# A two-block transformer on one core: ScalarE splits the second weight panel of the next stage ahead of a norm's squares or root instead of behind its root

## The reference

```python
def first_block(x, ...):                 # "a" in the kernel
    for l in range(2):
        h = rmsnorm(x, g_mix[l]); z = h @ w_in[l]          # attention, retention, gates
        x = x + mixed @ w_out[l]
        h2 = rmsnorm(x, g_mlp[l])
        x = x + square(relu(h2 @ w_up[l])) @ w_down[l]
    return rmsnorm(x, g_final)

def second_block(x, ...):                # "b" in the kernel
    for l in range(2):
        y = hybrid_mixer(x, ...)                           # sparse attention, gated linear attention
        x = layer_norm(DN_ALPHA * x + y, ln1_g[l], ln1_b[l])
        y = conv_ffn(x, w_up_2[l], conv_w[l], conv_b[l], w_down_2[l])
        x = layer_norm(DN_ALPHA * x + y, ln2_g[l], ln2_b[l])
    return x
```

## Time and profile before

| | |
|---|---|
| time, median of 3 runs | 3656.37 us (3656.33 to 3658.37) |
| profiled execution: time, span | 3656.84 us, 3655.0 us |
| TensorE matmul busy | 3461.4 us (95%) |
| ScalarE, VectorE, GpSimd busy | 1434.5, 1582.4, 1452.4 us (39, 43, 40%) |
| mean granted TensorE clock | 0.977 |

### The profile page before, as it was taken

One profiled execution on the slowest core, in us unless ns is written; L12 is line 12 of the kernel. 1 busy time (PEld: TensorE's weight loads), 2 busy tenths in 40 slices (PEclk: granted clock), 3 DMA queues, 4 the chain that ended last, 5 costly groups with the idle time before them and its releaser, 6 DMA issues.

```text
span 3655.0 us, 45462 instructions
## 1 busy us (share of the span) xinstructions
PE 3461.4 (95%) x16338; PEld 2807.0 (77%) x16338; DVE 1582.4 (43%) x2423; ACT 1434.5 (39%) x2116; POOL 1452.4 (40%) x1100
## 2 busy tenths in 40 slices
PE   7999999999999999999889999999897899999997
PEld 5788778887788778887668876787676688767875
DVE  5624242226623432237842444434577414344345
ACT  4735232224734332323363444333343524343333
POOL 3334444444334444444313343444332233434442
PEclk9999999999999999999999999999998999999999
DMA  3122222222112222222112221222221121212221
GB/s 139 58 74 77 92 92 93 93 103 81 70 70 93 92 82 102 92 98 78 70 35 73 69 93 70 92 97 98 72 78 58 44 72 70 93 58 96 99 92 58
DMA packets 43812, 298.49 MB, mean 82 GB/s; under 512 B 4816, under 2 KB 5456, under 8 KB 8592
## 3 DMA queue, kind: packets, MB, share of 16 engines
q1 hardware_dynamic: 41696, 291.52, 22.3%
q10 hardware_dynamic: 1968, 4.94, 0.4%
HBM read 294.34 MB, written 2.10 MB: 81 GB/s over the span
## 4 chain that ended last, share of the span: by engine, by line
issue 56%; POOL 33%; PE 8%; DVE 1%; ACT 1%; POOLq 1%; DVEq 0%; ACTq 0%
POOL w_lo L310 33%; PE ps L424 3%; PE ps L426 3%; PE ps L425 3%; POOLq L305 0%; PE ps L506 0%; DVE arena L1627 0%; ACT arena L1100 0%; POOLq L309 0%; DVE x L1662 0%; DVE arena L1650 0%; ACT y_hi L1119 0%; DVE tmp L1455 0%; ACT x L1418 0%; DVE x L1899 0%
## 5 line engine op out<-in xcount | busy, mean ns | idle before, releaser
L310 POOL TENSOR_TENSOR w_lo<-w_raw,w_hi 128x512 fp32r<-128x512 f32 x1096 | 1452.2, 1357 | 2161.0 <-ACT w_hi L924 2161.0
L424 PE MATMUL ps<-x_hi,w_hi 128*128 128x512 f32 x2752 | 1095.9, 398 | 20.6 <-DVE x_lo L1440 15.7
L426 PE MATMUL ps<-x_hi,w_lo 128*128 128x512 f32 x2752 | 1078.8, 392 | 0.0
L425 PE MATMUL ps<-x_lo,w_hi 128*128 128x512 f32 x2752 | 1077.8, 392 | 0.0
L924 ACT ACTIVATE w_hi<-w_raw 128x1024 fp32r<-128x1024 f32 x548 | 547.6, 1048 | 509.3 <-PE ps L426 509.3
L424 PEld LDWEIGHTS ps<-x_hi,w_hi 128*128 128x128 f32 x2752 | 521.4, 189 | 148.9 <-issue 24.3
L426 PEld LDWEIGHTS ps<-x_hi,w_lo 128*128 128x128 f32 x2752 | 520.1, 189 | 110.7
L425 PEld LDWEIGHTS ps<-x_lo,w_hi 128*128 128x128 f32 x2752 | 521.3, 189 | 106.7 <-issue 2.4
L424 PE MATMUL ps<-y_hi,w_hi 128*128 128x512 f32 x1248 | 493.4, 395 | 19.5 <-DVE x L1662 13.0
L425 PE MATMUL ps<-y_lo,w_hi 128*128 128x512 f32 x1248 | 489.3, 392 | 0.0
L426 PE MATMUL ps<-y_hi,w_lo 128*128 128x512 f32 x1248 | 488.8, 392 | 0.0
(11 more groups left out here) (184 smaller groups left out, 3153.5 us busy)
## 6 DMA issues: line engine op xcount, KB each, us to landing
w_raw<-stream SPq DMA_DIRECT2D x274, 1024.0 KB, 4.8
x<-x_t SPq DMA_DIRECT2D x4, 512.0 KB, 5.5
rotary<-rot ACTq DMA_DIRECT2D x4, 512.0 KB, 3.6
y_t<-x SPq DMA_DIRECT2D x8, 256.0 KB, 2.1
ct<-consts ACTq DMA_DIRECT2D x2, 770.0 KB, 4.9
arena<-pos ACTq DMA_DIRECT2D x2, 256.0 KB, 3.5
vec<-vectors ACTq DMA_DIRECT2D x4, 116.0 KB, 2.0
ct<-consts ACTq DMA_DIRECT2D x1, 128.0 KB, 3.9
```

What stands on the lines that cost most here:

```text
L310: ins = nc.gpsimd.tensor_tensor(WL[:, s, c:c + S], RAW[:, s, c:c + S], WH[:, s, c:c + S].bitcast(F32), ALU.subtract)
L424: pe.matmul(ps, wh, xh, start=(k == 0), stop=False)
L425: pe.matmul(ps, wh, xl, start=False, stop=False)
L426: return pe.matmul(ps, wl, xh, start=False, stop=last)
```

## The change

In `norm` (first block, five places) `hi(second_panel)` moves from behind `token_root` to ahead of it. In the layer norms (second block, three places: the fourth has no next stage) `hi` of the second panel moves from behind `root` to ahead of the eight squares. No instruction is added or removed; VectorE's, TensorE's, GpSimd's and SyncE's programs are the same.

```diff
@@ -1161,8 +1161,8 @@
                     const_dma(act, CT[:, 256:CW], consts_in[0, :, 256:CW], "consts_a")
                     hi(0)
                 warm_root()
+                hi(second_panel)
                 token_root(bank, (t, l, which + "_ms"), (t, l, which + "_root"))
-                hi(second_panel)
                 for k in range(KD):
                     src = X[:, k, :] if to_x else TMP[:, k % 2, :]
@@ -1405,13 +1405,13 @@
                 for which, gain in (("ln1", VB["ln1_g"]), ("ln2", VB["ln2_g"])):
+                    if which == "ln1" or l + 1 < DEPTH:
+                        hi(w["ff"] + 1 if which == "ln1" else at_b(l + 1)["iq"] + 1)
                     for _ in squares(lambda k: X[:, k, :], KD, lambda k: TMP[:, k % 2, :], lambda k: (t, l, which + "_centered", k),
                             lambda k: (t, l, which + "_ms", k - 2) if k >= 2 else None, (t, l, which + "_sq")):
                         pass
                     warm_root()
                     root(PS[:, 5, :], D, LN_EPS, (t, l, which + "_root"), [(t, l, which + "_ms"), "eps"])
-                    if which == "ln1" or l + 1 < DEPTH:
-                        hi(w["ff"] + 1 if which == "ln1" else at_b(l + 1)["iq"] + 1)
                     for k in range(KD):
```

## The result

| | median, us | runs | lowest to highest |
|---|---|---|---|
| before | 3656.35 | 12 | 3654.75 to 3661.80 |
| changed | 3665.98 | 12 | 3664.03 to 3668.14 |

A forecast was written before the change was run, and what follows sets the result against it. It took the ScalarE-VectorE chain on which TensorE waits in the nine norms as the bound. RMS norms +5.7 and layer norms -1.2 gave +4.5 us, so 3660.9 us, 0.12% above, range 3656.5 to 3666.0.

The forecast's parts named there:

- the x_lo at 0.69 us: RMS norms from the second on: x_lo start after GpSimd is through and lose their stalls, 0.24 to 1.02 us.
- the freed scalings: Layer norms: scalings no longer beside GpSimd, first gain-and-bias 0.73 us behind the first scaling instead of 1.84; 1.11 gained each.
- the longer sum: Layer norms: one of VectorE's last two sums, now beside GpSimd, longer by 0.5 to 0.9 us.
- Later root: Five RMS norms: the split ahead delays ScalarE's root by 1.99 us less the gap it fills; sum 5.0 us.
- GpSimd beside the diagonal: RMS norms: GpSimd starts ahead of VectorE's diagonal and stretches it, by 0.62 to 0.88 us in the second to fifth.
- rule of thumb: VectorE instructions with two SBUF inputs end about 0.2 us behind a GpSimd piece's end, about 0.55 behind the last.
- Net of the RMS norms, +5.7: Five RMS norms: root delay plus stretched diagonal less freed x_lo: 1.5, 2.0, 0.95, 0.7, 0.55; sum +5.7 us.
- My third rival: RMS norms: longer TensorE waits bring the lower clock into the next stage's first matmuls; total +9.0, 3665.4 us; chance 0.13.
- Layer norms, -1.2: Three layer norms: each gains 1.11 us at the scaling, loses 0.7 at the sums; -0.4 each, -1.2 us together.
- Outside the norms, 0: Stages behind the norms: full of matmuls, give nothing back; earlier load of the panel after next worth nothing.
- My first rival: Layer norms: second sum not stalled and clock stays up, -4.8 us there; total +0.9, 3657.3 us; chance 0.16.
- The second (a blocked instruction is blocked whole): Five diagonals and three sums beside GpSimd end 0.5 us later each; total +8.5, 3664.9 us; chance 0.08.

The follow-up runs named there:

- e2: Only the layer norms' part of the change (three places), against the kernel before: 3658.50 us, ratio 0.9996.
- e5: The kernel before with four idle copies on ScalarE ahead of the very first root: 3659.23 us, ratio 1.0006 against before.
- e8: The changed kernel with VectorE's diagonal made by four 128x128 multiplications by a per-partition number: 3673.47 us, ratio 1.0043 against before.
- e1: Only the RMS norms' part of the change (five places), against the kernel before: 3666.48 us, ratio 1.0019.
- e3: RMS norms only: split ahead of the root, but GpSimd let go only after the diagonal, against the kernel before: 3658.50 us, ratio 1.0000.
- e4: Layer norms only, the split ahead of the squares waiting for VectorE's last sum, against the kernel before: 3649.60 us, ratio 0.9973.
- e6: The kernel before with eight idle copies on ScalarE ahead of the very first root: 3663.30 us, ratio 1.0016 against before.
- e7: The changed kernel with four instead of eight dummy matmuls behind the spread in RMS norms: 3666.67 us, ratio 1.0020 against before.
- e11: The gated layer norms (e4) with four idle copies in the first norm: 3656.22 us, ratio 0.9991 against before.
- e9: The kernel before with two idle ScalarE copies ahead of the root of each of the five RMS norms: 3670.31 us, ratio 1.0026 against before.
- e10: The changed kernel with four idle copies ahead of the first split: 3670.52 us, ratio 1.0029 against before.
- e12: The changed RMS norms with the gated layer norms of e4: 3663.50 us, ratio 1.0008 against before.

## Why the prediction was right or wrong

The direction, the chain and the range were right (3660.9 forecast, 3656.5 to 3666.0; measured 3665.98). That the range held was luck: it held by 0.02 us, and the kernel lost 9.6 us where I had 4.5. The most likely class was not: I gave 0.78 to a time within 0.2%, and the kernel is slower by 0.24%. Of the signs that the prediction named, the stretched diagonal at four places, the x_lo at 0.69 us, the freed scalings and the longer sum came as said; the granted clock did not stay (0.977, then 0.972). By steps:

- **Later root, 5.0 us.** The mechanism is right; the term was too large. The root now stands 2.00 us behind `warm_root`, where before it stood 0.30, 0.81, 1.89, 1.11 and 1.83: 4.1 us later.
- **GpSimd beside the diagonal.** Right in kind, too small. I had 0.62 to 0.88 us at four places; it is 1.08 at each (1.77 against 0.69). My rule of thumb (0.2 us behind a piece's end, 0.55 behind the last) came from taking the pieces as equal. They are 1.26 us long, and 1.71 where one waited for VectorE, and by their own ends the 0.55 holds at every place, in the rows of before too. The diagonal starts at the start of a piece and so waits it out almost whole: 1.22 + 0.55 - 0.69 = 1.08. The two errors cancel, since the end of a GpSimd piece sets the diagonal's end however early the root is: counted from `warm_root` it ends 2.25, 1.19, 1.95 and 1.23 us later in the second to fifth norm, and my sums of root and stretch said 2.23, 1.19, 1.70 and 1.21. In the first norm the diagonal got shorter (0.82 instead of 1.29), and I had 0.6 too much.
- **Net of the RMS norms, +5.7.** Measured +6.6. What was missing is that in the third to fifth norm dummies at 1.2 GHz held up the first product, by 1.5 us in all (somewhat less is left at the panel's end). My third rival had looked for the clock in the products; it sat in the dummies ahead of them.
- **Layer norms, -1.2.** The gain of 1.11 us at a place was exact (1.12, and 3.7 us over three with the clock). The loss at the sums was 0.95 and 0.92 instead of 0.7. The mean's longer wait also met the lower clock once: the second layer norm is 0.9 us longer, not shorter. Net -0.4 (in e2's trace -1.2, what I had).
- **Outside the norms, 0.** This step failed. "The stages behind are full of matmuls and give nothing back" took it that they cost nothing either. The trace has 5.1 us there; with 6.6 and -0.4 for the norms, 3.4 of the median's 9.6 are left for it. 4.6 of the 5.1 are the second block's first mixer, and over the fourteen traces its length goes with TensorE's time at the lower clock in it: 563.2 us with 27 us of it (e2, e5), 563.3 and 563.4 with 31 (e8, before), 565.1 to 566.6 with 34 (e1, e3, e4, e6, e7, e11), 567.9 to 568.1 with 41 (the changed kernel, e9, e10, e12). So the clock goes with the mixer's length at every kernel, and its size fits: 10 us more at half the clock are worth up to 5 us.

That longer RMS norms bring this about is not shown. The seven kernels with the old RMS norms or only a later root (before, e2 to e6, e11) have 3418.1 to 3421.0 us outside the norms (mean 3419.2), the seven others 3421.0 to 3426.1 (mean 3423.5). But the executions profiled in the first group lay 1.9 us below their kernels' medians on average and those in the second 0.3 above, so that about half of the 4.3 us may be the choice of executions; and e8, with the longest RMS norms of all (138.8), has 3421.0 us outside and the short mixer.

My first rival (no stall of the sums) is refuted by 2.37 us for two sums. The second (a blocked instruction is blocked whole) had the mechanism more nearly than my sum: the instruction waits for the whole piece and then ends 0.55 us behind it, not 0.69. Its size was too large, since it set 0.5 us on top of a sum that took the pieces as too long: it asked for a mean stall of 1.2 us, and the eight places show 0.9 (0.13 in the first norm's diagonal, 1.08 in four, 0.92 to 0.95 in three sums). That its total of 3664.9 lies near the result is chance, as the rest came from the mixer.

What stays open is why this mixer has more of the lower clock in the changed kernel (the shift between the two traces grows some 140 to 170 and 250 to 340 us into it). e9 shows that GpSimd's place isn't needed for it; e5 and e6 that one delay at the start did not bring it about, e10 that one did not take it away; e1, with the same RMS norms as the changed kernel, has 565.1 us. One trace for each kernel does not tell a rule from chance.

## What to carry to other kernels

An instruction moved off a chain costs something where its followers on another engine land: here the two copies ahead of the root cost 3.0 us in the norms (e3), and the four GpSimd subtractions that they set free 3.5 more, because they fell beside a VectorE instruction with two inputs in SBUF. Place such work beside VectorE instructions that read PSUM (0.67 to 0.75 us for 128x512 beside GpSimd in all fourteen traces), and gate it there if it could start earlier: e4, whose one wait is all that it has beyond e2, is 0.27% below before, though e11 and e12 keep only a part of that. In a kernel with many short gaps in TensorE's work, a few microseconds of chain move the spells of the lower clock in stages that were not touched, so that an edit worth 0.1 to 0.2% has to be judged at more than one phase, and by more than one trace.

## What the runs showed that I had not expected

- VectorE and GpSimd take turns: a VectorE instruction of 128x512 with two inputs in SBUF ends 0.54 to 0.56 us behind the end of the GpSimd piece beside which it started, at all 148 to 162 places of each trace, and the GpSimd piece that starts meanwhile takes 1.71 to 1.77 us instead of 1.26.
- A VectorE tensor_scalar of 128x128 beside GpSimd's subtractions takes 1.30 us (median of the 20 in e8), its shortest 0.27.
- Unchanged code differs from kernel to kernel: the second RMS norm takes 21.1 to 22.9 us where its own code is as before, the second block's first mixer 563.2 to 568.1.
- Four dummy matmuls fewer (e7) made the next 9 to 11 products run at 1.2 GHz in three of five norms.
